# The second norm, moved from a stage of its own into the first output projection

## The chip, the cores and the metric

The kernel runs on 1 core of one Trainium2 chip. The metric is the device time of one execution in microseconds; several executions are run and their median is taken.

## The reference

Two blocks of a model, one after the other, on a sequence of 2048 rows of width 1024. The place that matters is the seam between them:

```
mix = concatenate([dn, sw], axis=-1)             # 2048 x 1024, delta rule and windowed attention
x1  = x + mix @ w_out                            # end of the first block
h   = rmsnorm(x1, norm_g)                        # start of the second block
proj = h @ w_in2                                 # 1024 -> 6144 columns
...                                              # chunked attention, convolution, gates
return rmsnorm(x1 + m @ w_out2, final_norm_g)
```

All is float32. Each product is done as three passes over a rounded part (`hi`) and the rest (`lo`): hi·hi, hi·lo, lo·hi.

## The kernel before, in words

The program is a chain of stages (blocks) that run one after the other on all engines; at the end of a block all engines meet, its semaphores are cleared, and the next begins. Each engine follows its own list of instructions and waits on semaphores. The order of the work is written out by hand.

`mix_output` (tiles `mo_*`) is the first output projection. It works on 16 tiles of 128 rows, two buffers of each tile. For a tile, GpSimd adds the two directions of the delta rule, squares them, and gates the window attention; VectorE and ScalarE norm, weight and gate the rows into `mix`; TensorE turns `mix` by 4 transposes (`turn`) into `pt`; ScalarE rounds it into `mhi` (`split_hi`); VectorE takes the rest into `mlo` (`split_lo`); TensorE does 48 products of 512 columns into `pp`; VectorE adds `x`; SyncE stores the row tile to `x1` in memory and loads the next `x`. ScalarE issues the five loads of rows three tiles ahead (`load_rows`, two of `delta_o`, one each of `gate_rows`, `sw_fm`, `gate_fm`) between its `split_hi` and its `root`. VectorE's order in a step is `split_lo(i+1)`, `rows(i+2)`, the sum of `pp` and `x` for tile i.

`norm_combine` (tiles `n_*`) is the second norm. It reads `x1` back, norms each row tile (a square with its sum on ScalarE, a root, a reciprocal, one scaling on VectorE into `xs`), turns it by 8 transposes of TensorE, and joins two tiles that stand 512 rows apart (a pair) into the 7 forms `A11, A12, A22, S1, S3, S2, S4` of a seven-product matrix scheme. Four pairs (`STORED`, the second half of the sequence) go to memory in `h_later`, 1792 KB each. The other four (`KEPT`) are for the first half. All pass through a buffer `cb`, two of them, and are rounded into `chi` and `clo` (the trace's `h_hi`, `h_lo`). It also loads the first weights and splits the first of them.

`project_second` (tiles `pj_*`) is the projection that follows: 24 units of 2 x 512 rows-by-columns blocks, each unit 7 steps of 12 products. Its first product of a unit, `B11`, uses form `A11`. For unit 0, ScalarE and VectorE split the weights of the 7 steps ahead of their accumulating work.

Of the kernel before, what the change touches and what calls it, by code (L numbers as in the profile page):

```python
# [27 lines left out]
F32 = mybir.dt.float32  # L28
# [1849 lines left out]
def attention(nc, name, warm, n_warm, consts, load_tile, n_kt, bias_of, bias_shape, load_bias, sink_rows, lanes, shapes, span, deep, out,  # L1878
# [14 lines left out]
    with Ctx(nc, name, USED) as c:  # L1893
# [4 lines left out]
        kr = c.sb("kr", [P, nk_tiles, SEQ])  # L1898
        vr = c.sb("vr", [P, TILES, vw])
        neg = [c.sb(f"neg{k}", [P, kp]) for k in SLOTS]  # L1900
        pr = [[c.sb(f"pr{r}{k}", [P, kp]) for k in SLOTS] for r in S]
# [89 lines left out]
        def _(sp):  # L1991
# [7 lines left out]
            if later:  # L1999
                w_out, delta_o, gate_rows, norm_row, ident_src = later.sources  # L2000
                for s in S:
                    for d in range(2):
                        sp.dma_start(later.of[s][:, d, :], delta_o[d, s]).then_inc(delta_in[s], 16)
# [9 lines left out]
            if later:  # L2013
# [3 lines left out]
                for s in S:  # L2017
                    sp.dma_start(later.gate[s][:], gate_rows[s]).then_inc(row_const_in, 16)
# [281 lines left out]

class MixAhead:


    def __init__(self, nc, stack, w_out, delta_o, gate_rows, norm_row, consts):
# [4 lines left out]
        self.raw = sb("raw", [P, KT, DM])  # L2309
        self.whi = sb("whi", [P, KT, DM], F32R)  # L2310
        self.wlo = sb("wlo", [P, KT, DM], F32R)
# [13 lines left out]
def mix_output(nc, delta_o, sw_fm, gate_rows, gate_fm, ahead, x, out, warm):  # L2325

    W = DN_W  # L2330
    with Ctx(nc, "mo", USED) as c:
        S = range(2)
        ident, wrow, whi, wlo = ahead.ident, ahead.wrow, ahead.whi, ahead.wlo
        of, gate, st = ahead.of, ahead.gate, ahead.st
        mix = [c.sb(f"mix{s}", [P, W]) for s in S]
# [4 lines left out]
        mlo = [c.sb(f"mlo{s}", [P, KT, P], F32R) for s in S]  # L2340
        pt = [c.ps(f"pt{s}", [P, W]) for s in S]
# [3 lines left out]
        names = ("rows_in x_in summed2 squared summed eps_added rooted inverted normed weighted gated sw_gated turned hi_ready lo_ready product added stored").split()  # L2345
        m = {n: c.sems(n, 2) for n in names}
        block = c.open_block()
        H = TILES // 2

        def load_rows(eng, j, t):  # L2350

            i, s, u = of_pair(j, t)
            for d in range(2):
                eng.dma_start(of[s][:, d, :], delta_o[d, i]).then_inc(m["rows_in"][s], 16)
            eng.dma_start(gate[s][:], gate_rows[i]).then_inc(m["rows_in"][s], 16)
            load_window(eng, j, t)

        def load_window(eng, j, t):
            i, s, u = of_pair(j, t)
            at = bass.ds(i * P, P)  # L2360
# [3 lines left out]
        def load_x(sp, j, t):  # L2364
            i, s, u = of_pair(j, t)
            sp.dma_start(xin[s][:], x[i]).then_inc(m["x_in"][s], 16)

        @block.sync
        def _(sp):
            def step(j, t, follow):  # L2370
                i, s, u = of_pair(j, t)
                sp.wait_ge(m["added"][s], u + 1 + START)
                sp.dma_start(out[i], xin[s][:]).then_inc(m["stored"][s], 16)
                if follow > 1:
                    sp.wait_ge(m["stored"][s], 16 * u + 16 + START)
                    load_x(sp, j, t + 2)

            for t in range(2):
                load_window(sp, 0, t)
            for t in range(2):  # L2380
                load_x(sp, 0, t)
            tile_pairs(sp, step)
            for s in S:
                sp.wait_ge(m["stored"][s], 16 * H + START)

        @block.gpsimd
        def _(pool):
            for s in S:
                pool.wait_ge(m["rows_in"][s], 32 + START)
                nc.gpsimd.tensor_tensor(sw[s][:], sw[s][:], gsw[s][:], ALU.mult).then_inc(m["sw_gated"][s], 1)  # L2390
            with pool.Fori(1, H) as j:
                for s in S:
                    pool.wait_ge(m["rows_in"][s], 80 * j + 32 + START)
                    nc.gpsimd.tensor_tensor(of[s][:, 0, :], of[s][:, 0, :], of[s][:, 1, :], ALU.add).then_inc(
                        m["summed2"][s], 1)
                    pool.wait_ge(m["summed2"][s], j + START)
                    nc.gpsimd.tensor_tensor(of[s][:, 1, :], of[s][:, 0, :], of[s][:, 0, :], ALU.mult).then_inc(
                        m["squared"][s], 1)
                    nc.gpsimd.tensor_tensor(sw[s][:], sw[s][:], gsw[s][:], ALU.mult).then_inc(m["sw_gated"][s], 1)

        @block.vector
        def _(dve):
            def rows(j, t):

                i, s, u = of_pair(j, t)
# [7 lines left out]
                scale_rows(j, t)  # L2413

            def scale_rows(j, t):
                i, s, u = of_pair(j, t)
# [14 lines left out]
            def split_lo(j, t):  # L2431
                i, s, u = of_pair(j, t)
# [6 lines left out]
            def step(j, t, follow):  # L2439
                i, s, u = of_pair(j, t)  # L2440
                if follow > 0:
                    split_lo(j, t + 1)
                if follow > 1:
                    rows(j, t + 2)
                dve.wait_ge(m["product"][s], u + 1 + START)
                dve.wait_ge(m["x_in"][s], 16 * u + 16 + START)
# [1285 lines left out]
```

## Time and profile before

| | us |
|---|---|
| median of 3 runs | 3168.65 |
| the 3 runs | 3168.65, 3153.8, 3176.06 |
| the profiled execution, its own time | 3165.56 |
| its span | 3163.8 |
| TensorE busy in the span | 2940.3 (93%) |
| VectorE / ScalarE / GpSimd busy | 1795.2 / 1283.3 / 551.5 |

The mean granted TensorE clock of that execution is 0.971 of full speed. The profiled execution's time is the span plus 1.8 us around it. Busy times are of each engine by itself; the stage is what counts, since the stages follow one another.

### The profile page before, as it was taken

The numbers are of one execution on the slowest core, as the hardware profiler recorded it, in microseconds if no ns is written. First come the engines' busy times: TensorE is split into PE (matmuls) and PEld (weight loads), VectorE is DVE, ScalarE is ACT, GpSimd is POOL, SyncE is SP. The second block draws the span as 40 slices with busy tenths as digits, with TensorE's granted clock in tenths as the row PEclk, the third lists the DMA queues.
The fourth block names the chain that finished last, engine by engine and source line by source line (L and its number), as shares of the span: only waits on it lengthen the run. The fifth ranks groups of instructions, "written<-read, shape, count | busy, mean of one in ns | idle before, by whom it ended". The sixth has DMA issues, their size and how long they took to land. (4 is left out here: it accounts for less than half of the span.)

```text
span 3163.8 us, 56622 instructions
## 1 busy us (share of the span) xinstructions
PE 2940.3 (93%) x21119; PEld 2408.9 (76%) x21139; DVE 1795.2 (57%) x3274; ACT 1283.3 (41%) x2752; POOL 551.5 (17%) x475
## 2 busy tenths in 40 slices
PE   7998999997999989899599999999999899989998
PEld 6886998775888866688388888878888666668787
DVE  5755443074877857554755775665775455543433
ACT  5221433154665569410523223433223377730232
POOL 0000000062343400132032232342332100000000
PEclk9999999999998999999799999999999999999999
DMA  4221775154666532354633223443223362145443
GB/s 141 80 80 73 247 256 200 52 153 161 198 199 192 157 113 98 113 203 153 228 107 107 70 70 117 160 140 106 65 71 116 114 199 88 30 158 207 173 146 119
DMA packets 302666, 431.96 MB, mean 137 GB/s; under 512 B 43600, under 2 KB 181072, under 8 KB 296784
## 3 DMA queue, kind: packets, MB, share of 16 engines
q1 hardware_dynamic: 253936, 392.40, 37.5%
q10 hardware_dynamic: 48480, 36.18, 3.6%
q8 instruction: 162, 2.65, 0.3%
q14 instruction: 88, 0.72, 0.1%
HBM read 279.01 MB, written 149.49 MB: 135 GB/s over the span
## 5 line engine op out<-in xcount | busy, mean ns | idle before, releaser
L114 PE MATMUL pj_pp<-h_hi,pj_whi 128*128 128x512 f32 x1152 | 449.9, 391 | 6.9 <-POOL h_lo L3121 6.9
L115 PE MATMUL pj_pp<-h_lo,pj_whi 128*128 128x512 f32 x1152 | 448.7, 390 | 0.0
L116 PE MATMUL pj_pp<-h_hi,pj_wlo 128*128 128x512 f32 x1152 | 448.7, 389 | 0.0
L114 PEld LDWEIGHTS pj_pp<-h_hi,pj_whi 128*128 128x128 f32 x1152 | 216.6, 188 | 52.8 <-issue 8.1
L2948 ACT CAST pj_whi<-w_raw 128x512 fp32r<-128x512 f32 x192 | 119.1, 622 | 327.1 <-PE pj_pp L116 318.5
L116 PEld LDWEIGHTS pj_pp<-h_hi,pj_wlo 128*128 128x128 f32 x1152 | 216.6, 188 | 45.0
L115 PEld LDWEIGHTS pj_pp<-h_lo,pj_whi 128*128 128x128 f32 x1152 | 216.7, 188 | 44.8
L3012 DVE TENSOR_TENSOR pj_wlo<-w_raw,pj_whi 128x512 fp32r<-128x512 f32 x192 | 159.7, 832 | 11.6 <-ACT pj_whi L2948 8.6
L114 PE MATMUL np_pp<-h_hi,np_whi 128*128 128x512 f32 x384 | 150.4, 392 | 0.0
L116 PE MATMUL np_pp<-h_hi,np_wlo 128*128 128x512 f32 x384 | 149.7, 390 | 0.0
L115 PE MATMUL np_pp<-h_lo,np_whi 128*128 128x512 f32 x384 | 149.7, 390 | 0.0
L3141 POOL TENSOR_TENSOR w_raw<-w_raw,pj_t 128x512 f32<-128x512 f32 x48 | 62.7, 1306 | 441.6 <-DVE pj_wlo L3012 441.6
L2948 ACT CAST pj_whi<-pj_t 128x512 fp32r<-128x512 f32 x96 | 59.6, 621 | 173.7 <-PE pj_pp L116 155.0
L1689 POOL TENSOR_TENSOR gr_sw<-gr_tab,gr_wrow 128x64 f32<-128x64 f32 x32 | 15.7, 521 | 641.8 <-DMA gr_ident<-in_consts 641.8
L2227 ACT ACTIVATE ca_pr<-ca_neg,ca_nmx 128x640 f32<-128x640 f32 (+4 forms) x128 | 97.7, 763 | 67.3 <-DVE ca_nmx L2167 67.3
L2167 DVE CUSTOM_DVE_ANT_0 ca_neg<-ca_s,ca_bias 128x640 f32<-128x640 f32 (+4 forms) x128 | 89.8, 739 | 51.1 <-PE ca_s L2051 49.5
L345 DVE SCALAR_TENSOR_TENSOR np_acc<-np_pre,np_taps,np_acc 128x2048 f32<-128x2048 f32 (+3 forms) x60 | 115.5, 1926 | 2.1
L114 PE MATMUL mo_pp<-ahead_whi,mo_mhi 128*128 128x512 f32 x256 | 103.3, 404 | 0.5 <-DVE mo_mlo L2451 0.5
L115 PE MATMUL mo_pp<-ahead_wlo,mo_mhi 128*128 128x512 f32 x256 | 101.9, 398 | 0.0
L116 PE MATMUL mo_pp<-ahead_whi,mo_mlo 128*128 128x512 f32 x256 | 101.9, 398 | 0.0
L114 PE MATMUL fo_pp<-fo_whi,fo_mhi 128*128 128x512 f32 x256 | 99.8, 390 | 0.0
L116 PE MATMUL fo_pp<-fo_whi,fo_mlo 128*128 128x512 f32 x256 | 99.6, 389 | 0.0
(415 smaller groups left out, 7174.4 us busy)
## 6 DMA issues: line engine op xcount, KB each, us to landing
w_raw<-in_w_second SPq DMA_DIRECT2D x192, 256.0 KB, 2.8
ds_pk<-scratch_pack SPq DMA_DIRECT2D x64, 384.0 KB, 4.6
scratch_pack<-rp_out SPq DMA_DIRECT2D x32, 512.0 KB, 2.7
ds_pk<-scratch_pack SPq DMA_DIRECT2D x64, 256.0 KB, 3.7
scratch_sig_fm<-pj_ob SPq DMA_DIRECT2D x64, 256.0 KB, 2.2
mb_sg<-scratch_sig_fm SPq DMA_DIRECT2D x16, 1024.0 KB, 7.7
rp_fm<-scratch_qkv_fm SPq DMA_DIRECT2D x96, 128.0 KB, 2.8
scratch_qkv_fm<-np_acc SPq DMA_DIRECT2D x11, 1024.0 KB, 4.8
```

The source lines that it names most:

```text
L114: nc.tensor.matmul(out, ah, bh, start=(first and i == 0), stop=False)
L115: nc.tensor.matmul(out, ah, bl, start=False, stop=False)
L116: mm = nc.tensor.matmul(out, al, bh, start=False, stop=(last and i == n - 1))
L345: nc.vector.scalar_tensor_tensor(out=acc[s][:, at], in0=pre[s][:, at.start + t:at.stop + t], scalar=taps[:, n, t:t + 1], in1=acc[s][:, at] ...
L1689: ins = nc.gpsimd.tensor_tensor(sw[s][:, :, k, a:a + HH], tab[s][:, 1, :, a:a + HH], wrow[:, k, b:b + HH].unsqueeze(1).to_broadcast([P, 2, ...
L2167: nc.vector.tensor_tensor_reduce(neg[k][:, 0:n * P], s_ps[k][:, 0:n * P], bias_of(bias, h)[:, b0:b0 + n * P], -scale, sink[:, 1, h:h + 1] ...
L2227: nc.scalar.activation(pr[q % 2][k][:, 0:n * P], neg[k][:, 0:n * P], ACT.Exp, bias=nmx[s][:, h:h + 1], scale=-1.0, accum_out=den[s][:, 0, ...
L2948: nc.scalar.copy(whi[i], raw_of[i]).then_inc(hi_ready[i], 1)
L3012: nc.vector.tensor_tensor(wlo[i], raw_of[i], whi[i].bitcast(F32), ALU.subtract).then_inc(lo_ready[i], 1)
L3141: nc.gpsimd.tensor_tensor(raw[1][0], raw[1][0], t2[:], ALU.subtract).then_inc(t4_ready, 1)
```

## The change

`mix_output` and `norm_combine` become one block, `mix_and_norm`. The row tiles are taken in a new order, `ROW_ORDER`, so that two tiles 512 rows apart follow each other, the second half of the sequence first. Each tile of x1 is squared, rooted and scaled from the sum that stands in `xin`, and TensorE turns it in the step after its own, between the 36th and the 37th product. The sum of `pp` and `x` is made in two halves. There is one `xs`, one `nt` in PSUM and one `cb`. `S2` and `S4` go from VectorE to GpSimd. The kept pairs are written in full precision into `combos`, and no longer rounded there, but for `A11`; the other six forms are rounded in `project_second`, ahead of the first unit, with half of the rest on GpSimd. All loops over tiles are written out. Large tiles of the stages share a hand-placed region (`Arena`), in which the window attention before has its tiles too.

```diff
-def mix_output(nc, delta_o, sw_fm, gate_rows, gate_fm, ahead, x, out, warm):
-def norm_combine(nc, name, x, norm_row, consts, chi, clo, later, w_first, w_raw, w_split, warm):
+ROW_ORDER = [8 * half + p + 4 * e for half in (1, 0) for p in range(4) for e in range(2)]
+def mix_and_norm(nc, delta_o, sw_fm, gate_rows, gate_fm, ahead, arena, x, norm_row, w_first, later, out, warm):
+    STORED_PAIRS = H // 2
...
+        xs = c.sb("xs", [P, DM])
+        cb = c.sb("cb", [P, N_COMB, K4W, P])
+        nt = c.ps("nt", [P, KT, P])
...
+        def forms(u, k):
+            return cb[:, k] if u < STORED_PAIRS else combos[:, k, place(u)]
         @block.sync
+            def store_forms(u):
+                sp.wait_ge(low_ready, u + 1 + START)
+                sp.wait_ge(s4_ready, u + 1 + START)
+                sp.dma_start(later[:, :, place(u)], cb[:]).then_inc(later_stored, 16)
+            def step(i):
+                s, u = i % 2, i // 2
+                if i >= 3 and i % 2 and (i - 3) // 2 < STORED_PAIRS:
+                    store_forms((i - 3) // 2)
                 sp.wait_ge(m["added"][s], u + 1 + START)
+                sp.dma_start(out[ROW_ORDER[i]], xin[s][:]).then_inc(m["stored"][s], 16)
+                if i + 2 < TILES:
+                    sp.wait_ge(xs_ready, i + 1 + START)
                     sp.wait_ge(m["stored"][s], 16 * u + 16 + START)
+                    load_x(i + 2)
         @block.gpsimd
+            def last_forms(u):
+                pool.wait_ge(s1_ready, u + 1 + START)
+                pool.wait_ge(top_ready, u + 1 + START)
+                nc.gpsimd.tensor_tensor(forms(u, S2), forms(u, S1), forms(u, A11), ALU.subtract).then_inc(s2_ready, 1)
+                pool.wait_ge(s2_ready, u + 1 + START)
+                nc.gpsimd.tensor_tensor(forms(u, S4), forms(u, A12), forms(u, S2), ALU.subtract).then_inc(s4_ready, 1)
+            for i in range(2, TILES):
...                                  # sum, square and gate of tile i, as before
+                if i % 2 and i >= 5:
+                    last_forms((i - 5) // 2)
+            last_forms(H - 2)
+            last_forms(H - 1)
         @block.vector
+            def low_forms(u):
+                dve.wait_ge(row_turned, 2 * u + 2 + START)
+                dve.wait_ge(a22_ready, u + 1 + START)
+                nc.vector.tensor_tensor(forms(u, S1), nt[:, 0:K4W, :], forms(u, A22), ALU.add).then_inc(s1_ready, 1)
+                dve.wait_ge(top_ready, u + 1 + START)
+                nc.vector.tensor_tensor(forms(u, S3), forms(u, A11), nt[:, 0:K4W, :], ALU.subtract).then_inc(low_ready, 1)
+            def norm(i):
...                                  # scale and epsilon, wait for the root, reciprocal, then
+                nc.vector.scalar_tensor_tensor(out=xs[:], in0=xin[s][:], scalar=nst[:, 3:4], in1=nrow[:], op0=ALU.mult,
+                                               op1=ALU.mult).then_inc(xs_ready, 1)
+            def step(i):
+                if i >= 3 and i % 2:
+                    low_forms((i - 3) // 2)
+                if i + 1 < TILES:
+                    split_lo(i + 1)
+                if 1 <= i <= TILES:
+                    norm(i - 1)
+                if i + 2 < TILES:
+                    rows(i + 2)
+                if i < TILES:
+                    add_x(i)
...
+            for h in S:              # after step(TILES + 1)
...
+                nc.vector.tensor_tensor(clo[:, A11, 2 * h:2 * h + 2], combos[:, A11, 2 * h:2 * h + 2],
+                                        chi[:, A11, 2 * h:2 * h + 2].bitcast(F32), ALU.subtract)
         @block.scalar
+            def copy_row(i):
+                u = i // 2
+                act.wait_ge(row_turned, i + 1 + START)
+                if i % 2 == 0:
+                    if 0 < u <= STORED_PAIRS:
+                        act.wait_ge(later_stored, 16 * u + START)
...                                  # A11 and A12 of pair u out of nt
+                else:
+                    nc.scalar.copy(forms(u, A22), nt[:, K4W:KT, :]).then_inc(a22_ready, 1)
+            def step(i):
+                if i >= 2:
+                    copy_row(i - 2)
+                if i + 1 < TILES:
+                    split_hi(i + 1)
+                if 1 <= i <= TILES:
+                    square(i - 1)
+                if i + 3 < TILES:
+                    act.wait_ge(m["lo_ready"][(i + 1) % 2], (i + 1) // 2 + 1 + START)
+                    load_rows(act, i + 3)
+                if 1 <= i <= TILES:
+                    norm_root(i - 1)
+                if i + 2 < TILES:
+                    root(i + 2)
         @block.tensor
+            def turn_row(i):
+                u = i // 2
+                pe.wait_ge(xs_ready, i + 1 + START)
...                                  # and top_ready or low_ready, then 8 transposes of xs into nt
+            def step(i):
+                s, u = i % 2, i // 2
+                if i + 1 < TILES:
+                    turn(i + 1)
                 pe.wait_ge(m["lo_ready"][s], u + 1 + START)
                 pe.wait_ge(m["added"][s], u + START)
+                products(i, 0, range(0, KT)).then_inc(half_product, 1)
+                products(i, NCOL, range(0, 4))
+                turn_row(i - 1)
+                products(i, NCOL, range(4, KT)).then_inc(m["product"][s], 1)
...
+            pe.wait_ge(m["half_added"][0], H + START)
+            keep_warm(nc, pp[0][:, 0:NCOL], warm, 20)
+            turn_row(TILES - 1)
 def project_second(...):
         # ScalarE, ahead of the first unit
             for i in range(1, STEPS):
+                for h in S:
+                    nc.scalar.copy(chi[:, A_OF[i], 2 * h:2 * h + 2], combos[:, A_OF[i], 2 * h:2 * h + 2]).then_inc(first_hi, 1)
                 split_hi(i, 0)
         # VectorE
             for i in range(1, STEPS):
+                for h in S if i == 1 else S[0:1]:
+                    dve.wait_ge(first_hi, 2 * (i - 1) + h + 1 + START)
...                                  # clo of that half
                 split_lo(i, 0)
         # GpSimd, first unit: the other half of clo
+            def first_low_of(i):
+                pool.wait_ge(first_hi, 2 * i + START)
...
+                if u == 0:
+                    for i in range(2, 4):        # after t1, t2, t3
+                        first_low_of(i)
+                if u == 0:
+                    for i in range(4, STEPS):    # after t4
+                        first_low_of(i)
         # TensorE, step(u, i)
+                if u == 0 and i > 0:
+                    pe.wait_ge(first_lo, i + 1 + START)
+                if u == 0 and i > 1:
+                    pe.wait_ge(first_low, i - 1 + START)
```

## Rows read from the trace of the kernel before

**Rows 1.** Stretches: length; busy PE, PEld, DVE, ACT, POOL; TensorE clock, DMA share, GB/s.

```profile
1327.00:1503.00 176.00, 176.00 (x776) 142.88 (x774) 83.63 (x121) 18.16 (x41) 49.17 (x39) 0.98 0.51 176
...
1512.00:1585.40 73.40, 40.74 (x213) 25.52 (x214) 59.12 (x79) 44.06 (x71) 3.75 (x3) 0.78 0.65 226
```

**Rows 2.** Timeline of VectorE and TensorE at both ends of the norm stage (start, length).

```profile
1503.13 1.22 DVE L2447 TENSOR_TENSOR mo_xin<-mo_pp,mo_xin 128x1024 f32<-128x1024 f32 x1 [9.91 <-PE mo_pp L116]
...
1577.29 1.22 DVE L2685 TENSOR_TENSOR h_lo<-n_cb,h_hi 128x1024 fp32r<-128x1024 f32 x1
...
1585.40 0.58 PE L114 MATMUL pj_pp<-h_hi,w_hi 128*128 128x512 f32 x1
```

**Rows 3.** Groups of instructions, 1500 to 1590 (busy us, mean ns; idle before, releaser).

```profile
L2673 DVE SCALAR_TENSOR_TENSOR n_xs<-n_x,n_stat,n_wrow 128x1024 f32<-128x1024 f32 x16 | 19.8, 1282 | 0.3
L2727 PE MATMUL n_pt<-n_ident,n_xs 128*128 128x128 f32 x128 | 19.3, 301 | 17.9 <-DVE n_xs L2673 17.8
L2625 ACT ACTIVATE n_xs<-n_x 128x1024 f32<-128x1024 f32 x16 | 16.9, 1059 | 31.3 <-DMA n_x<-scratch_x 31.1
...
L2649 ACT COPY n_cb<-n_pt 128x1024 f32<-128x1024 f32 x8 | 8.0, 1000 | 5.1 <-DMA scratch_h_later<-n_cb 3.3 <-DVE h_lo L2679 1.8
...
L2701 DVE TENSOR_TENSOR n_cb<-n_pt,n_cb 128x512 f32<-128x512 f32 x8 | 5.5, 687 | 2.3 <-ACT n_cb L2654 2.1
...
L2679 DVE TENSOR_TENSOR h_lo<-n_cb,h_hi 128x1024 fp32r<-128x1024 f32 x4 | 4.9, 1219 | 0.0
```

**Rows 4.** Timeline of a steady step of the projection, engine by engine (ACTq: issues).

```profile
1399.04 0.60 PE L2499 MATMUL mo_pt<-ahead_ident,mo_mix 128*128 128x128 f32 x4
1399.40 0.48 PE L114 MATMUL mo_pp<-ahead_whi,mo_mhi 128*128 128x512 f32 x1
...
1410.64 0.60 PE L2499 MATMUL mo_pt<-ahead_ident,mo_mix 128*128 128x128 f32 x4
...
1399.34 1.23 DVE L2447 TENSOR_TENSOR mo_xin<-mo_pp,mo_xin 128x1024 f32<-128x1024 f32 x1 [2.80 <-PE mo_pp L116]
...
1400.16 0.62 ACT L2472 CAST mo_mhi<-mo_sw 128x512 fp32r<-128x512 f32 x1
...
1402.29 0.87 ACTq L2354 DMA_DIRECT2D ahead_of<-scratch_delta_o  x2
...
1404.80 0.20 ACT L2464 ACTIVATE ahead_st<-ahead_st 128x4 f32<-128x4 f32 x1 [4.01 <-issue]
...
1406.70 0.69 DVE L2429 TENSOR_TENSOR mo_mix<-mo_mix,ahead_gate 128x512 f32<-128x512 f32 x1
...
1413.10 1.20 DVE L2436 TENSOR_TENSOR mo_mlo<-mo_sw,mo_mhi 128x512 fp32r<-128x512 f32 x1
```

**Rows 5.** DMA issues: 1300 to 1600, then two stores by themselves (KB, us to landing).

```profile
scratch_h_later<-n_cb SPq DMA_DIRECT2D x4, 1792.0 KB, 7.3
...
scratch_h_later<-n_cb SPq DMA_DIRECT2D x1, 1792.0 KB, 9.0
...
scratch_h_later<-n_cb SPq DMA_DIRECT2D x1, 1792.0 KB, 6.4
```

**Rows 6.** Timeline: TensorE behind three of its waits, and VectorE after the first.

```profile
1326.70 1.11 PE L2499 MATMUL mo_pt<-ahead_ident,mo_mix 128*128 128x128 f32 x4 [4.36 <-DVE mo_mix L2429]
...
1341.28 1.23 DVE L2447 TENSOR_TENSOR mo_xin<-mo_pp,mo_xin 128x1024 f32<-128x1024 f32 x1 [4.87 <-PE mo_pp L116]
...
2064.18 0.47 PE L114 MATMUL pj_pp<-h_hi,pj_whi 128*128 128x512 f32 x1 [2.85 <-POOL h_lo L3121]
...
2070.11 0.76 PE L114 MATMUL pj_pp<-h_hi,pj_whi 128*128 128x512 f32 x1 [2.96 <-POOL h_lo L3121]
```

**Rows 7.** Stretches of 1 and 4 us behind those waits (columns as in Rows 1).

```profile
1331.00:1332.00 1.00, 1.00 (x4) 0.78 (x3) 0.76 (x2) 0.00 (x0) 0.00 (x0) 0.50 0.44 61
...
2070.00:2074.00 4.00, 3.89 (x10) 3.11 (x11) 1.42 (x3) 0.62 (x1) 3.92 (x3) 0.58 0.36 126
```

**Rows 8.** Instructions of one line, GpSimd on 1024 columns (min/median/max ns).

```profile
L3121 POOL TENSOR_TENSOR h_lo<-pj_araw,h_hi x7: 2344/2399/3260, 2033.1 to 2067.6; 128x1024 fp32r<-128x1024 f32 x7
```

More of the change, by code:

```diff
@@ L2017, in _ @@
                 for s in S:
-                    sp.dma_start(later.gate[s][:], gate_rows[s]).then_inc(row_const_in, 16)
+                    sp.dma_start(later.gate[s][:], gate_rows[ROW_ORDER[s]]).then_inc(row_const_in, 16)
                 sp.wait_ge(raw_in, 16 + START)
@@ L2380, in _ @@
-            for t in range(2):
-                load_x(sp, 0, t)
-            tile_pairs(sp, step)
+                    load_x(i + 2)
+                if i == TILES - 4:
+                    for r in S:
+                        for q in S:
+                            sp.dma_start(w_raw[r][q], w_first[q][:, r * K4W:(r + 1) * K4W, :]).then_inc(
+                                w_ahead if r or q else w0_in, 16)
+            for i in range(2):
+                load_window(sp, i)
+            for i in range(2):
+                load_x(i)
@@ L2488, in _, with turn @@
             act.wait_ge(m["lo_ready"][0], 1 + START)
-            load_rows(act, 0, 2)
-            tile_pairs(act, step, peel=2)
+            load_rows(act, 2)
+            for i in range(TILES + 2):
+                if i == TILES - 1:
+                    act.wait_ge(w0_in, 16 + START)
+                    nc.scalar.copy(w_split[0], w_raw[0][0]).then_inc(w0_hi, 1)
+                if i == TILES + 1:
+                    for s in S:
+                        act.wait_ge(m["product"][s], H + START)
+                    for h in S:
+                        nc.scalar.copy(chi[:, A11, 2 * h:2 * h + 2], combos[:, A11, 2 * h:2 * h + 2]).then_inc(a11_hi, 1)
+                step(i)
         @block.tensor
         def _(pe):
-            def turn(j, t):
-                i, s, u = of_pair(j, t)
+            def turn(i):
+                s, u = i % 2, i // 2
                 pe.wait_ge(m["gated"][s], u + 1 + START)
@@ L2519, in _ @@
                 if ks.start:
-                    turn(0, 1)
+                    turn(1)
                     pe.wait_ge(m["lo_ready"][0], 1 + START)
                 for a in (0, NCOL):
-                    mm = split_products(nc, pp[0][:, a:a + NCOL],
-                                        [(mhi[0][:, k, :], mlo[0][:, k, :], whi[:, k, a:a + NCOL],
-                                          wlo[:, k, a:a + NCOL]) for k in ks], first=ks.start == 0, last=ks.stop == KT)
+                    mm = products(0, a, ks)
@@ L2731 @@
+            for i in range(1, TILES):
+                step(i)
+            pe.wait_ge(m["half_added"][0], H + START)
+            keep_warm(nc, pp[0][:, 0:NCOL], warm, 20)
+            turn_row(TILES - 1)
 STEPS = 7
@@ L2741, in second_units, with project_second @@
     return ["qk"] * 4 + ["v"] * 2 + ["z"] * 2 + conv + ["sig"] * 8
-def project_second(nc, w_tiles, conv_w, consts, chi, clo, later, raw, w_split, qk, v_rows, z, yconv, sig, warm):
+def project_second(nc, w_tiles, conv_w, consts, combos, chi, clo, later, raw, w_split, qk, v_rows, z, yconv, sig, warm):
     KINDS = second_units()
@@ L3573, in build @@
     x1 = scratch("x1", [TILES, P, DM])
-    with ExitStack() as held:
-        ahead = MixAhead(nc, held, d["w_out1"], delta_o, gate_rows, d["dn_norm"], d["consts"])
-        if stage("wa"):
-            window_attention(nc, d, rope_fm, proj_rows, sw_fm, ahead, warm)
-        if stage("mix"):
-            mix_output(nc, delta_o, sw_fm, gate_rows, gate_fm, ahead, d["x"], x1, warm)
     h_later = scratch("h_later", [P, N_COMB, 4, K4W, P])
```

449 lines of the change are left out of this document (175 added, 274 removed).

## The prediction

> **What bounds the kernel now.** I read the busy shares first, then stretches cut at the borders of the stages, then the timeline of one steady step, then the waits. In the output projection TensorE is busy for the whole of 1327 to 1503, 176.00 of 176.00 us; VectorE has 83.63, ScalarE 18.16 and GpSimd 49.17 [rows 1]. So there anything that costs TensorE no time is free, and what it must do or wait for is paid in full. In the norm stage TensorE is not the bound: VectorE is busy for 59.12 of 73.40 us and ScalarE for 44.06, and part of TensorE's 40.74 is only there to keep it warm [rows 1]. Between VectorE's last sum of the projection (1503.13) and the first product of the next one (1585.40) lie 82.3 us [rows 2]. This is all that the change can win. Its price is paid in the projection before and at the border behind.
>
> **The border, after.** Time 0 is the start of the last half sum, at the place of 1503.13. Half sum 0.7 (as a form of 512 columns, 0.69); square 1.06 and the read-out of its sum [rows 3], to 2.0; scale and epsilon, root (0.20 [rows 4]), reciprocal, with the hand-overs to 2.65; scaling into `xs` 1.28 [rows 3], to 3.95. Twenty warming products cover TensorE until about 4.4. Eight transposes 0.9, to 5.3. ScalarE has rounded the two halves of `A11` meanwhile (two of 1.0, off the path) and copies `A22`, 0.6, to 5.95. VectorE makes `S1` and `S3`, 0.69 each less their overlap [rows 3], to 7.25, then two rests of `A11`, 1.22 each [rows 3], to 9.7; GpSimd's `S2` and `S4` end with it (1.3 each, a little over half of its 2.40 for 1024 columns [rows 8]). From the end of the last rest (1577.29 + 1.22) to the first product there are 1585.40 - 1578.51 = 6.9 us [rows 2], a change of stage that I keep. So 16.6 us in place of 82.3: **-65.7**.
>
> **Eight transposes in each step.** Four transposes take 0.36 us to the next product (1399.04 to 1399.40); that product stands 0.08 longer, and the step is 1410.64 - 1399.04 = 11.60 us, so 48 products stand 0.234 apart [rows 4]. Eight cost 2 x 0.36 + 0.08 = 0.8; the upper bound is the norm stage's 19.3 / 16 = 1.2 us a tile, part of them at a low clock [rows 3]. I take 0.9. Fifteen lie inside the projection (the last is in the border): **+13.5** (12 to 18). The step becomes 12.5 us, and the transposes are wanted 0.44 + 36 x 0.234 = 8.8 us after its start.
>
> **Is `xs` there by then?** In a step, counted from its first transpose: the half sum is done at 1.0 (the sum starts at 0.30 now), ScalarE's two casts end at 1.75 [rows 4], its square at 2.9. VectorE's two rests end at 3.1; beside a gate of GpSimd's, the second is 1.20 instead of 0.69 [rows 4], and they end at 3.7. In every second step `S1` and `S3` come first, 1.3 us, of which 0.7 was idle: 4.1. Only then does ScalarE issue its five loads, 1402.29 to the root at 1404.80, 2.5 us [rows 4], and behind those stands the root of the second norm. Issues end at 5.7 to 6.8, root and reciprocal at 6.2 to 7.3, `xs` at 7.5 to 8.7. So it is in time, by 0.1 to 1.3 us. Behind it on VectorE stand the rows of tile i+2, reduce to gate: some 4.1 us: now the root starts at 1404.80 and the gate ends at 1407.39, 2.6 us on [rows 4]; reduce, scale and the root itself before it are 1.5. They end at 11.6 to 12.8 where the step ends at 12.5. The steps with `S1` and `S3` are the tight ones, seven of them, 0.3 us each: **+2** (0 to 6).
>
> On the extra subtractions of GpSimd the Trainium skill speaks against the change: its page "GPSIMD Engine Reference", section "8. Key points", has GpSimd contend with VectorE instructions that have two SBUF inputs. The 1.20 us beside 0.69 agrees. By that rule the scaling into `xs` (two SBUF inputs) would also grow if `S2` and `S4` last into it, to about twice, and seven steps would lose up to 1 us more each; the forecast holds without it.
>
> **Where I see the largest cost: one `cb`.** Pair u is complete in step 2u+3, and `copy_row` of pair u+1 is the first thing that ScalarE does in step 2u+4; it waits for the store of pair u. The store is SyncE's, and behind `load_x` of tile 2u+4, which waits for `xs` of tile 2u+2, made in step 2u+3 at 7.5 to 8.7. GpSimd's `S4` is done at 6.5 to 8. So the store is issued at about 8.8, with 512 KB of x just ahead and row loads in flight. Landing took 6.4 us by itself and 9.0 with loads of x beside it, median 7.3 [rows 5]. I take 8.5: 17.3, which is 4.8 into step 2u+4. Before, there were two buffers, and such a wait came to 3.3 us in all [rows 3]. Queued behind it on ScalarE stand the copy (1.0), the casts of tile 2u+5, the square, the five issues and the root; `xs` is ready 8.05 behind the landing, at 12.85, and TensorE wants it at 8.8. It waits 4.05 us.
>
> **And its clock.** After a wait of 4.36 us, four transposes took 1.11 instead of 0.60 us, and the stretch at 1331 still shows half the clock (1.2 GHz); the step took 1341.28 - 0.30 - 1326.70 = 14.3 us, 2.7 more than 11.60 [rows 4, 6, 7]. After one of 2.85 us the next product still took 0.47; after one of 2.96, 0.76 and a clock of 0.58 in that stretch [rows 6, 7]. So a wait of 4 us most likely brings the low clock, and I add 2.5. This happens for pairs 1, 2, 3 and 4, in steps 4, 6, 8 and 10: 4 x (4.05 + 2.5) = **+26.2**. Ends: landing in 6.4 leaves waits of 2 us and no loss of clock, 8; landing 2.5 later than I take gives 4 x 9.3 = 37.
>
> **The first unit behind.** In `project_second`, ScalarE rounds two halves of a form (1.0 each [rows 3]) and a weight (0.62 [rows 4], less the overlap) for each of six steps, 2.5 us a step where TensorE needs 12 x 0.234 = 2.8; VectorE has a rest of 1.22 and one of 0.69 [rows 3]. GpSimd's half rest is 2.40 us (up to 3.26) [rows 8], five of them and four weight sums of 1.3: with the wait of its fourth sum for `lo_ready` of B21 its last ends some 22.5 after the last rest before the border. TensorE starts at 6.9 and wants the last at 23.7. So there is 1.2 to spare; with the longer durations it is late by up to 4: **+1.5** (0 to 5).
>
> Nothing is won by the reads of x1 that fall away, since they lay in the stage that is gone. Loops written out, more semaphores, the new order and the shared memory I take at nothing: TensorE covers the first; without that cover they'd be tenths of a us.
>
> **The sum.** -65.7 + 13.5 + 2 + 26.2 + 1.5 = -22.5; 3165.56 - 22.5 = 3143 for a profiled execution. The median stands 3.1 above that execution, so I say 3146. The three runs spread by 0.35% to each side, so 1% (31.7 us) is about what can be told from no change.
>
> **Rivals.** A: the store lands early enough, or the clock stays up. Waits of 2 us instead of 4.05 and no low clock: +8 instead of +26, 3128; with the transposes at 0.8, 3126. For it: 6.4 us alone, and two of four stores of before were waited for little. Against: 0.5 MB ahead in the same queue. B: the steps without a store are late too, since `xs` has 0.1 us to spare in the worst of them. 1.5 us in each of eleven steps: +16.5, 3163. C, slower: ScalarE's five issues take 5 us instead of 2.5, as the queue is fuller by 1792 KB for two tiles. Then `xs` comes at 11 in every step, 2.3 us late and at the edge of the low clock: 11 x (2.3 + 2.5) + 4 x 2.3 = +62, 3208. It decides from issues of about 4.5 us; against it, they are 2.5 at a DMA share of 0.51 [rows 1, 4]. D: the change doesn't do what it says, and the border is only halved, to 41 us, because another thing than the last tile's chain (SyncE's wait for its stores or the first weights) opens the next stage: +24, 3170. Against: the last pair that is stored is done four tiles before the end, and a store of `x1` is 512 KB.
>
> Page "DMA: Bandwidth & Descriptors", section "Queues, rings and completion order", of the Trainium skill says that descriptors of a ring are consumed in order. By it the x load goes before the store, which alone would make 9.0 rather than 7.3; no row here shows the order itself.
>
> **Chances.** Forecast 0.50, A 0.25, B 0.13, C 0.08, D 0.04. Faster by over 1% (under 3137): most of A and a fifth of the forecast, 0.32. Slower by over 1%: C and little else, 0.09. Same: 0.59. The range goes from A with the low ends of the other terms (3123, and 5 less for the spread of the runs) to B with a high end of the store's term (3174).
>
> **What would show it.** Right: ScalarE's copy of `A11` waits for the DMA of `h_later` four times, some 5 us; TensorE's transposes out of `xs` wait for VectorE behind it, some 4 us, with a clock near 0.5 after; steps of 12.5 us otherwise; 16 to 17 us from the last sum to the first product. Wrong: waits in all steps (B, C), or none (A). I'd be wrong most easily by the landing of the store, on which 29 us hang.

## The result, and the profile after

| | before | after |
|---|---|---|
| median, 6 runs each | 3159.66 us | 3133.11 us |
| ratio, 95% interval | 1 | 0.9918 (0.989 to 0.9946) |
| profiled execution (span) | 3165.56 (3163.8) | 3128.35 (3126.6) |

The change made the kernel 26.5 us faster, 0.8% (17 to 35 us by the interval). Run twice more below, it came out 18.4 and 25.7 us below the kernel before. The forecast was 22.5 less than before; its absolute figure, 3146, started from a median of three runs of 3168.65, where six runs give 3159.66. The two profiled executions are 37 us apart, but 9.7 us of that had arisen before the stage that the change rewrites: the first product of the projection starts at 1310.45 in the one and at 1300.79 in the other. Ahead of it the change touches only where the tiles of the window attention stand, and in the second run of the changed kernel the same product starts at 1310.80. So what follows compares stretches with known ends, not spans.

The steps of the projection come first, as the timeline of TensorE shows them (`turn` is L2677, `turn_row` L2688). They answer to [rows 4].

```profile
1343.08 0.60 PE L2677 MATMUL mo_pt<-ahead_ident,mo_mix 128*128 128x128 f32 x4
1351.88 1.03 PE L2688 MATMUL mo_nt<-ahead_ident,mo_xs 128*128 128x128 f32 x8
1355.55 0.60 PE L2677 MATMUL mo_pt<-ahead_ident,mo_mix 128*128 128x128 f32 x4
1368.57 1.97 PE L2688 MATMUL mo_nt<-ahead_ident,mo_xs 128*128 128x128 f32 x8 [4.06 <-DVE mo_xs L2555]
1374.97 0.60 PE L2677 MATMUL mo_pt<-ahead_ident,mo_mix 128*128 128x128 f32 x4
...
1387.47 0.60 PE L2677 MATMUL mo_pt<-ahead_ident,mo_mix 128*128 128x128 f32 x4
1399.76 1.09 PE L2688 MATMUL mo_nt<-ahead_ident,mo_xs 128*128 128x128 f32 x8 [3.31 <-DVE mo_xs L2555]
1405.02 0.66 PE L2677 MATMUL mo_pt<-ahead_ident,mo_mix 128*128 128x128 f32 x4 [1.39 <-DVE mo_mix L2530]
```

Step 3 (1343.08 to 1355.55) is 12.47 us, 0.87 more than 11.60. Its transposes out of `xs` start 8.80 after its own start and wait for nothing. Step 4 is 19.42: 4.06 of waiting for `xs`, then transposes at 1.97 instead of 1.03, which is half the clock (0.50 granted), and half-speed products behind. Step 6 is 17.55: 3.31 of waiting, no fall of the clock, and 1.39 of waiting at its end for the mix of tile 8. Steps 8 and 10 are 18.96 and 18.07, with waits of 3.66 and 3.82. In step 10 the transposes still take 1.09, and the clock falls only behind them:

```profile
1461.76 1.09 PE L2688 MATMUL mo_nt<-ahead_ident,mo_xs 128*128 128x128 f32 x8 [3.82 <-DVE mo_xs L2555]
...
1463.57 0.63 PE L114 MATMUL mo_pp<-arena_whi,mo_mhi 128*128 128x512 f32 x1
...
1466.80 0.39 PE L116 MATMUL mo_pp<-arena_whi,mo_mlo 128*128 128x512 f32 x1
```

The granted clock is 0.50 from 1464 to 1466, and the step loses 1.8 us beyond its wait (18.07 - 12.47 - 3.82). So a look at the first instructions behind a wait isn't enough to say that the clock stayed up. The four steps stand 24.1 us above four ordinary ones: 14.8 of waiting for `xs`, 7.9 behind the waits (2.89, 0.38, 2.83 and 1.78), 1.4 of waiting for the mix. The eight ordinary steps from 2 to 13 are 12.46 to 12.52.

The waits of the whole stretch, 1290 to 1560 (us in total, times, longest), tell who is late for whom.

```profile
ACT mo_cb L2623 <- DMA scratch_h_later<-mo_cb: 26.3, 3, 8.9
...
PE mo_nt L2688 <- DVE mo_xs L2555: 14.9, 4, 4.1
...
ACT arena_combos L2623 <- DMA scratch_h_later<-mo_cb: 9.0, 1, 9.0
```

ScalarE stands four times for the store of the pair before, 35 us in all, where it stood for 3.3 before [rows 3]; TensorE waits 14.9 us behind that. In step 6 the chain is this, from the timelines of SyncE (steps 3 and 4), ScalarE and VectorE.

```profile
1351.12 0.33 SPq L2442 DMA_DIRECT2D mo_xin<-in_x  x1
1351.55 0.61 SPq L2447 DMA_DIRECT2D scratch_h_later<-mo_cb  x1
...
1392.21 1.01 ACT L2623 COPY mo_cb<-mo_nt 128x1024 f32<-128x1024 f32 x1 [8.63 <-DMA scratch_h_later<-mo_cb]
1393.12 0.59 ACT L2612 CAST mo_mhi<-mo_pt 128x512 fp32r<-128x512 f32 x1
...
1395.59 0.82 ACTq L2429 DMA_DIRECT2D ahead_of<-scratch_delta_o  x2
...
1397.98 0.20 ACT L2636 ACTIVATE mo_nst<-mo_nst 128x1 f32<-128x1 f32 x1 [2.70 <-issue]
...
1398.41 1.28 DVE L2555 SCALAR_TENSOR_TENSOR mo_xs<-mo_xin,mo_nst,mo_nrow 128x1024 f32<-128x1024 f32 x1
```

The store of pair 0 is issued 8.5 us into step 3, right behind the load of x; the one that step 6 waits for, of pair 1, is issued 8.0 into step 5 (1382.99). Four such stores landed 9.1 to 9.5 us after their issue (median 9.3), which answers to [rows 5]. In step 6 the copy starts at 1392.21, 4.7 into the step; the casts, the square, the five issues and the root follow in a row, and `xs` is there 7.5 us on.

The border to the next stage, VectorE and TensorE, answers to [rows 2].

```profile
1529.13 0.69 DVE L2565 TENSOR_TENSOR mo_xin<-mo_pp,mo_xin 128x512 f32<-128x512 f32 x1 [5.74 <-PE mo_pp L116]
...
1536.22 4.12 DVE L2598 TENSOR_TENSOR arena_clo<-arena_combos,arena_chi 128x1024 fp32r<-128x1024 f32 x2
...
1547.32 0.99 PE L114 MATMUL pj_pp<-arena_chi,arena_w_hi 128*128 128x512 f32 x1
```

It is 18.2 us from the last half sum to the first product, where 82.3 were. The two rests at its end took 4.12 us, not 2.4.

The first unit of `project_second` grew: its second unit starts at 1574.03, 26.7 us after its first, where it was 1604.67 - 1585.40 = 19.3. Groups of instructions from 1547 to 1574:

```profile
L3132 POOL TENSOR_TENSOR arena_clo<-arena_combos,arena_chi 128x1024 fp32r<-128x1024 f32 x5 | 14.3, 2881 | 1.4 <-ACT arena_chi L2976 1.4
L3076 DVE TENSOR_TENSOR arena_clo<-arena_combos,arena_chi 128x1024 fp32r<-128x1024 f32 x5 | 10.4, 2087 | 0.0
L114 PE MATMUL pj_pp<-arena_chi,pj_whi 128*128 128x512 f32 x24 | 10.3, 428 | 4.7 <-POOL arena_clo L3132 3.8 <-DVE pj_wlo L3014 0.9
...
L3014 DVE TENSOR_TENSOR pj_wlo<-arena_w_raw,pj_whi 128x512 fp32r<-128x512 f32 x4 | 7.9, 1980 | 0.2 <-ACT pj_whi L2948 0.2
```

Rests of 1024 columns took 2.09 us on VectorE on average (1.22 in [rows 3]) and 2.88 on GpSimd (2.40 in [rows 8]); the four rests of 512 columns that read `arena_w_raw` took 1.98 on average where 0.69 is their time alone. By the view of the whole stretch (1547.3 to 1574), VectorE was busy for 23.0 of 26.7 us and GpSimd for 21.7; TensorE waited 4.7 us and lost some more to the clock, which was 0.91 on average:

```profile
1547.30:1574.00 26.70, 22.00 (x86) 17.34 (x85) 23.00 (x14) 14.45 (x19) 21.73 (x11) 0.91 0.16 49
```

### The profile page after: what moved, and what is told of

It is laid out like the page before. It is cut to its first block and busy times, and to the rows that moved or that the text cites. A ratio compares the mean times of both kernels' runs of the same rounds, so it can differ in the third digit from the quotient of the medians.

```text
span 3126.6 us, 56243 instructions
## 1 busy us (share of the span) xinstructions
PE 2918.1 (93%) x21061; PEld 2395.2 (77%) x21077; DVE 1808.6 (58%) x3287; ACT 1284.8 (41%) x2762; POOL 589.8 (19%) x496
## 3 DMA queue, kind: packets, MB, share of 16 engines
q8 instruction: 166, 2.72, 0.4%
## 5 line engine op out<-in xcount | busy, mean ns | idle before, releaser
L114 PE MATMUL pj_pp<-arena_chi,pj_whi 128*128 128x512 f32 x1152 | 450.8, 391 | 8.5 <-POOL arena_clo L3132 3.8
L115 PE MATMUL pj_pp<-arena_clo,pj_whi 128*128 128x512 f32 x1152 | 449.5, 390 | 0.0
L116 PE MATMUL pj_pp<-arena_chi,pj_wlo 128*128 128x512 f32 x1152 | 449.3, 390 | 0.0
L114 PEld LDWEIGHTS pj_pp<-arena_chi,pj_whi 128*128 128x128 f32 x1152 | 216.9, 188 | 55.1 <-issue 10.4
L116 PEld LDWEIGHTS pj_pp<-arena_chi,pj_wlo 128*128 128x128 f32 x1152 | 217.1, 188 | 45.2
L115 PEld LDWEIGHTS pj_pp<-arena_clo,pj_whi 128*128 128x128 f32 x1152 | 217.2, 189 | 44.9
L2948 ACT CAST pj_whi<-arena_w_raw 128x512 fp32r<-128x512 f32 x192 | 119.2, 622 | 319.1 <-PE pj_pp L116 303.4
L3014 DVE TENSOR_TENSOR pj_wlo<-arena_w_raw,pj_whi 128x512 fp32r<-128x512 f32 x192 | 166.9, 869 | 9.8 <-ACT pj_whi L2948 7.1
L1689 POOL TENSOR_TENSOR gr_sw<-gr_tab,gr_wrow 128x64 f32<-128x64 f32 x32 | 15.8, 522 | 642.5 <-DMA gr_ident<-in_consts 642.5
L114 PE MATMUL mo_pp<-arena_whi,mo_mhi 128*128 128x512 f32 x256 | 106.5, 416 | 0.5 <-DVE mo_mlo L2582 0.5
L3014 DVE TENSOR_TENSOR arena_w_lo<-arena_w_raw,arena_w_hi 128x512 fp32r<-128x512 f32 x47 | 66.4, 1414 | 65.7 <-ACT arena_w_hi L2948 65.7
L116 PE MATMUL mo_pp<-arena_whi,mo_mlo 128*128 128x512 f32 x256 | 103.4, 404 | 0.0
```

The lines of the kernel that those rows point to most:

```text
L114: nc.tensor.matmul(out, ah, bh, start=(first and i == 0), stop=False)
L115: nc.tensor.matmul(out, ah, bl, start=False, stop=False)
L116: mm = nc.tensor.matmul(out, al, bh, start=False, stop=(last and i == n - 1))
L1689: ins = nc.gpsimd.tensor_tensor(sw[s][:, :, k, a:a + HH], tab[s][:, 1, :, a:a + HH], wrow[:, k, b:b + HH].unsqueeze(1).to_broadcast([P, 2, ...
L2948: nc.scalar.copy(whi[i], raw_of[i]).then_inc(hi_ready[i], 1)
L3014: nc.vector.tensor_tensor(wlo[i], raw_of[i], whi[i].bitcast(F32), ALU.subtract).then_inc(lo_ready[i], 1)
```

## The experiments

All kernels were run in five rounds against the kernel before. Each line below has its median, and its ratio to the kernel before with the interval.

| kernel | median us | ratio (95%) | long steps 4, 6, 8, 10 | first unit |
|---|---|---|---|---|
| the change again | 3141.36 | 0.9937 (0.9919 to 0.9954) | 19.3, 18.3, 15.8, 18.5 | 26.8 |
| four places | 3118.24 | 0.9861 (0.9833 to 0.9888) | 12.5 each | 28.4 |
| store first | 3121.85 | 0.9872 (0.985 to 0.9894) | 15.9, 15.0, 14.4, 15.1 | 26.7 |
| warmed waits | 3138.16 | 0.9925 (0.9908 to 0.9942) | 16.2, 17.6, 19.5, 16.9 | 26.5 |
| no fourth wait | 3132.67 | 0.9905 (0.988 to 0.993) | 17.3, 15.1, 18.3, 12.5 | 26.8 |
| root first | 3121.25 | 0.988 (0.9852 to 0.9907) | 14.7, 13.7, 13.7, 13.2 | 26.7 |
| turned twice | 3153.37 | 0.9978 (0.996 to 0.9996) | 18.6, 18.0, 17.8, 19.4 | 28.4 |
| rests on VectorE | 3133.04 | 0.9913 (0.9889 to 0.9936) | 18.4, 17.8, 17.4, 18.1 | 21.6 |
| the change, third time | 3137.56 | 0.9926 (0.9905 to 0.9946) | 16.2, 18.2, 17.8, 18.0 | 26.7 |
| S2, S4 on VectorE | 3143.70 | 0.9944 (0.9923 to 0.9965) | 20.1, 18.6, 20.2, 18.5 | 26.4 |
| combined | 3109.42 | 0.9853 (0.9828 to 0.9877) | 12.5 each | 23.9 |

The steps and the unit are read from the timeline of TensorE of one profiled execution each. Single steps differ by 1 to 3 us from one execution to the next of the same kernel, so the long steps are compared as a sum. The first unit is 26.4 to 28.4 in the ten executions whose code for it is that of the change.

**The change again.**

> The changed kernel again, as the reference for the three beside it. Four waits of TensorE for xs of 3 to 4 us in steps 4, 6, 8 and 10, some 24 us over four ordinary steps of 12.5 us; some 26 us faster than the kernel before.

The waits hold: four of 2.98 to 4.11 us for `xs`, 14.1 in all, and four steps 22.1 us above ordinary ones. The time does not: 18.4 us below the kernel before, not 26.

**Four places.**

```diff
-            return cb[:, k] if u < STORED_PAIRS else combos[:, k, place(u)]
+            return combos[:, k, place(u)]
...
-                    if 0 < u <= STORED_PAIRS:
-                        act.wait_ge(later_stored, 16 * u + START)
+                    if u >= STORED_PAIRS:
+                        act.wait_ge(later_stored, 16 * (u - STORED_PAIRS + 1) + START)
```

> The stored pairs are written into the four places of combos, which lie idle then, so that no pair waits for the store of the one before. Theory (the wait of ScalarE for the one cb makes the four long steps): no wait of TensorE for xs is left, steps 4, 6, 8 and 10 fall to 12.5 us, and the kernel is 24 us faster than the changed one. Rival (the long steps come from the load on VectorE and GpSimd, and the store only happens to stand there): waits of 2 us or more stay and it gains under 8.

It came out 23.1 us below the changed kernel of the same comparison (0.9861 against 0.9937, and the intervals are apart). Of TensorE's waits from 1340 to 1500 this is the whole list:

```profile
PE mo_pt L2677 <- DVE mo_mix L2530: 0.8, 1, 0.8
```

No wait for `xs` is left, and steps 3 to 13 are 12.46 to 12.68. The four long steps alone are 22.0 us shorter. The load on VectorE and GpSimd is the same, so the rival falls.

**Store first.** SyncE's order in a step:

```diff
-                if i >= 3 and i % 2 and (i - 3) // 2 < STORED_PAIRS:
-                    store_forms((i - 3) // 2)
                 sp.wait_ge(m["added"][s], u + 1 + START)
                 sp.dma_start(out[ROW_ORDER[i]], xin[s][:]).then_inc(m["stored"][s], 16)
+                if i >= 2 and i % 2 == 0 and (i - 2) // 2 < STORED_PAIRS:
+                    store_forms((i - 2) // 2)
```

> SyncE issues the store of pair u before it waits for xs and loads x of tile 2u+4; one cb as before. Theory (the landing counts from an issue that SyncE's own order holds back until xs is there): the issue moves from 8.3 to some 3 to 5 us after the start of step 2u+3, the landing by the same 4 us, and of the four long steps most of 24 us goes: 15 to 22 faster than the changed kernel. Rival (the landing is bound by the traffic of row loads, not by the issue): the landing takes as much longer as it starts earlier, and it gains under 5. x of tile 2u+4 now lands behind 1792 KB and might come late for the sum; then it is less.

19.5 us below the changed kernel by the medians. The four long steps account for 11.6 of it (60.4 us against 72.0), less than the forecast's 15 to 22; of the 15.1 us between the two profiled executions, 5.0 had arisen before the projection. SyncE's timeline in step 3, which starts at 1350.35 here, and ScalarE's copy in step 4, which starts at 1362.84:

```profile
1355.33 0.61 SPq L2447 DMA_DIRECT2D scratch_h_later<-mo_cb  x1
1358.54 0.33 SPq L2442 DMA_DIRECT2D mo_xin<-in_x  x1
...
1365.21 1.02 ACT L2623 COPY mo_cb<-mo_nt 128x1024 f32<-128x1024 f32 x1 [5.66 <-DMA scratch_h_later<-mo_cb]
```

The issue is at 5.0 in the step instead of 8.5, the landing takes 9.8 instead of 9.3 (medians), and the copy starts at 2.4 in step 4. The waits for `xs` fall to 0.98 to 1.82, and none brings the low clock; the mix is late at five steps' ends, 3.6 us in all. So SyncE's order alone held the store back by 3 to 3.5 us, and the landing took only 0.5 longer for it. The load of x behind the store landed after 8.0 us instead of 5.3, and VectorE didn't wait for it.

**Warmed waits.**

```diff
+                if i in (4, 6, 8, 10):
+                    pe.wait_ge(m["added"][1 - s], (i - 1) // 2 + 1 + START)
+                    keep_warm(nc, pp[1 - s][:, 0:NCOL], warm, 12)
                 turn_row(i - 1)
```

> Twelve warming products (2.7 us) in steps 4, 6, 8 and 10, in the place where TensorE waits for xs. The waits for xs stay (less 2.7 us each as idle time), and only the clock is different. Theory (two or three of the four waits bring the low clock, at 2 to 2.5 us each): 5 to 7 us faster than the changed kernel, no transposes of 1.97 us. Rival (the clock is not what lengthens those steps): no change, or up to 2 us slower where a wait is shorter than the warming.

3.2 us below the changed kernel, with intervals that overlap: by the times alone it is not settled. In the trace three of the four transposes behind the waits take 1.09 or 1.10 and one 1.97:

```profile
1398.36 1.09 PE L2688 MATMUL mo_nt<-ahead_ident,mo_xs 128*128 128x128 f32 x8 [1.53 <-DVE mo_xs L2555]
...
1429.84 1.97 PE L2688 MATMUL mo_nt<-ahead_ident,mo_xs 128*128 128x128 f32 x8 [2.80 <-DVE mo_xs L2555]
```

The forecast of 5 to 7 us is missed. What the steps lose beyond their waits falls from 8.0 us in the changed kernel beside it to 2.5, so the clock gave back some 5.5; but the idle times of this run and the warming in front of them (2.7 us) come to 16.2 us, 2.1 more than the waits beside it, and three waits for the mix at the steps' ends take 1.6. That the clock adds to the long steps is shown by the steps themselves. In the three runs of the changed kernel, nine of the twelve have a stretch at a granted clock of 0.50 and stand 1.6 to 3.0 us above an ordinary one beyond their waits; the three others stand 0.2 to 0.4 above it, as 15.84 - 12.47 - 3.15.

**No fourth wait.**

```diff
-                    if 0 < u <= STORED_PAIRS:
+                    if 0 < u < STORED_PAIRS:
```

> ScalarE's wait for the fourth store, in step 10, is left out: pair 4 goes to combos, not to cb, so nothing needs it. Theory: step 10 falls from 18 to 12.5 us and the other three stay, 5 to 6 us faster than the changed kernel. Rival (something else makes that step long): step 10 stays.

Step 10 is 12.46 in this run; the other three stay at 15 to 18. By the times it is 7 to 10 us faster than the changed kernel (0.9905 against 0.9926 and 0.9937), with intervals that overlap, so this is read from the step. A fourth of the cost stood for a wait that protects nothing.

**Root first.**

```diff
+                if 1 <= i <= TILES:
+                    norm_root(i - 1)
                 if i + 3 < TILES:
                     act.wait_ge(m["lo_ready"][(i + 1) % 2], (i + 1) // 2 + 1 + START)
                     load_rows(act, i + 3)
-                if 1 <= i <= TILES:
-                    norm_root(i - 1)
```

> ScalarE does the root of the second norm before it issues the five loads of rows, no longer behind them. Theory (ordinary steps have xs in time, and only the four long ones wait): xs comes 2.4 us earlier, which shortens the four waits by so much each and takes the low clock off some: 10 to 15 us faster than the changed kernel, ordinary steps still 12.5. Rival (the loads are what the rows of the next tiles wait for, and come later now): new waits for the rows in ordinary steps, no gain.

0.988, some 16 us below the changed kernel. The waits for `xs` are 1.99, 1.01, 1.04 and 0.46, and none brings the low clock; the four steps sum to 55.3 us instead of 72.0. One wait of 0.65 us for the mix appears, too small to count. Of the 16.7, 9.6 are the waits (4 x 2.4), and the rest is the clock, which stays up behind all four.

This run also shows what the landing hangs on. Three of its four stores are issued 10.5 to 11.0 us into their step, once GpSimd's `S4` is done, which is some 2.5 later than in the changed kernel and 4 to 5 behind the load of x. They land after 6.5 to 6.7 us, and ScalarE's copy starts 4.3 to 4.8 into the next step, no later than before. The first, issued 0.4 behind that load, takes 11.1. So an issue moved by itself does not move the landing by as much: what is in flight then counts too.

**Turned twice.**

```diff
-                for k in range(KT):
+                for k in list(range(KT)) * 2:
```

> Each row tile of x1 is turned twice, into the same place: 8 transposes more in each step. Theory (transposes are paid in full on TensorE at 0.09 to 0.1 us each): ordinary steps of 13.2 to 13.3 instead of 12.47, some 12 us slower than the changed kernel. Rival (TensorE has room in the steps): ordinary steps stay at 12.5.

```profile
1485.78 0.60 PE L2677 MATMUL mo_pt<-ahead_ident,mo_mix 128*128 128x128 f32 x4
1494.58 1.91 PE L2688 MATMUL mo_nt<-ahead_ident,mo_xs 128*128 128x128 f32 x16
1499.12 0.60 PE L2677 MATMUL mo_pt<-ahead_ident,mo_mix 128*128 128x128 f32 x4
```

Ordinary steps are 13.34, 0.87 above 12.47, and the kernel is at 0.9978, 13 to 16 us above the changed one. The eight transposes are paid in full, at the price of the forecast.

**Rests on VectorE.**

```diff
-                for h in S if i == 1 else S[0:1]:
+                for h in S:
...
-                if u == 0:
-                    for i in range(4, STEPS):
-                        first_low_of(i)
```

> In the first unit of project_second, VectorE makes both halves of the rests of the six forms, and GpSimd none of them. Theory (the two engines hold each other up on operations with two SBUF inputs, 3.4 instead of 1.2 us on VectorE and 3.0 instead of 2.4 on GpSimd, and that makes the unit 26.7 us instead of 19.3): the rests fall to 1.2 us, and the unit to 20 to 22 us, though VectorE has more work: 4 to 7 us faster than the changed kernel. Rival (the work is simply too much, wherever it is done): the unit stays at 26 or grows, as VectorE has five rests of 1.2 us more.

Groups from 1546.8 to 1568.5:

```profile
L3076 DVE TENSOR_TENSOR arena_clo<-arena_combos,arena_chi 128x1024 fp32r<-128x1024 f32 x10 | 11.7, 1212 | 0.0
```

And the view of one line, one of GpSimd's sums of the weights (minimum, median and longest in ns, first and last start in us):

```profile
L3152 POOL TENSOR_TENSOR arena_w_raw<-arena_w_raw,pj_t x48: 1284/1288/6215, 1557.5 to 2455.1; 128x512 f32<-128x512 f32 x48
```

VectorE does ten rests in 11.7 us where it did five in 10.4, and the unit falls from 26.7 to 21.6. The one sum of this line that falls into the stretch, the first of the 48, took 6.2 us where their median is 1.3, so the two engines still hold each other up; it is only no longer what TensorE waits for. The kernel is 4 to 8 us faster than the changed one by the ratios (0.9913), which the intervals alone don't separate; the unit's 5.1 is read from the trace. The 21.6 is clear of the 26.4 to 28.4 of the executions with the change's own code, and the rival (too much work wherever it is done) falls.

**The change a third time**, and beside it **S2, S4 on VectorE**.

> The changed kernel once more, as the reference for the two beside it: 0.8% faster than the kernel before.

```diff
                 nc.vector.tensor_tensor(forms(u, S3), forms(u, A11), nt[:, 0:K4W, :], ALU.subtract).then_inc(low_ready, 1)
+                nc.vector.tensor_tensor(forms(u, S2), forms(u, S1), forms(u, A11), ALU.subtract).then_inc(s2_ready, 1)
+                nc.vector.tensor_tensor(forms(u, S4), forms(u, A12), forms(u, S2), ALU.subtract).then_inc(s4_ready, 1)
```

> S2 and S4 are back on VectorE, right behind S1 and S3; GpSimd only gates the mix. Theory (VectorE's chain to xs has about 1 us to spare in a step with S1 and S3, 7.8 against 8.9): with 1.3 us more in front xs comes at 9.1, TensorE waits 0.3 us in seven ordinary steps, and the store, which is issued behind xs, lands later for the long steps: 2 to 6 us slower than the changed kernel. Rival (the rule that GpSimd and VectorE hold each other up on operations with two SBUF inputs decides): VectorE's operations beside S2 and S4 get shorter, the last two rests of the block fall from 2.1 to 1.2 us each, and it is 1 to 4 us faster.

Both theories are right in a part. The last two rests take what they take alone, as the rival said:

```profile
1547.53 2.35 DVE L2598 TENSOR_TENSOR arena_clo<-arena_combos,arena_chi 128x1024 fp32r<-128x1024 f32 x2
```

But the four waits for `xs` are 5.01, 4.33, 4.76 and 4.18, for the store is issued behind `xs` and that comes later (9.2 to 9.3 us into the step, not 8.0 to 8.5), and the kernel is at 0.9944, 6.1 us by the medians above the changed one beside it; the intervals overlap in part. No waits of 0.3 us in the steps with `S1` and `S3` appeared: those steps are 12.5 with an exception of 13.3 behind each of two long ones.

**Combined**: four places, root first, and rests on VectorE.

> Three edits together: the stored pairs in the four places of combos, the root ahead of the loads, and both halves of the first unit's rests on VectorE. Theory (the costs are separate, and with the first edit there is no wait that the second could shorten): -23 and -5 and 0, some 28 us faster than the changed kernel and 1.7% faster than the kernel before. Rival (they share one cover, or the root in front makes new waits): under 20.

28.1 us below the changed kernel beside it, as expected, and at 0.9853 the fastest of all. No step from 3 on is longer than 12.49. Its first unit is 23.9, not 21.6; TensorE waited 2.2 us in it instead of 1.6, and its granted clock there was 0.93 instead of 0.97. Four places alone were at 0.9861 in another comparison, so how much the other two edits add to it is not told apart.

## Why the prediction was right

The time fell by 26.5 us where 22.5 were forecast. The mechanism stands term by term, but for one term that was mis-sized:

| term | forecast | the profile after |
|---|---|---|
| border | -65.7 | 18.2 - 82.3 = -64.1 |
| fifteen times eight transposes | +13.5 | 15 x (12.47 - 11.60) = +13.1 |
| ordinary steps late | +2 | 0 |
| four long steps | +26.2 | +24.1 |
| first unit | +1.5 | +7.4 |
| sum | -22.5 | -19.5 |

**The border** was as worked out, but for 1.6 us: the two last rests stood beside GpSimd's `S4` and took 4.12 instead of 2.35, as the run with `S2` and `S4` on VectorE shows. The 6.9 us from the last rest to the first product were 7.0 (1547.32 - 1540.34).

**The transposes** cost what was taken, 0.87 a tile against 0.9; turning twice confirmed it.

**The slack in ordinary steps** was judged too small in two places. TensorE found `xs` ready in all of them, also with two more forms on VectorE in front: the trace has it at 7.8 us against 8.8 in step 7, where the forecast had up to 8.7. The +2 itself stood for the mix of the next tile, which was to end at up to 12.8 in a step of 12.5. In the steps with `S1` and `S3` it ended at 11.2 to 12.1, so nothing was paid in this execution; the third run of the change waited for it in two early steps, 0.74 and 0.32.

**The single `cb`** was the largest cost, and its chain held in each link: store issued at 8.0 to 8.5 (8.8 was forecast), landing after 9.3 (8.5), copy 4.7 to 5.5 into the step (4.8), `xs` 7.5 behind it (8.05), TensorE's wait 3.31 to 4.06 (4.05). Only the sign for ScalarE, waits of some 5 us, was off: it was free earlier and stood for 8.6 to 9.0. The edit that takes only this wait away gained 23.1 us; an earlier issue of the store gained 19.5, of which its long steps show 11.6, and a shorter queue behind the wait some 16. These are three ways to shorten one chain, and they don't add up. The forecast's 26.2 were 16.2 of waits and 10 of clock; measured were 14.8 of waits, 7.9 behind them and 1.4 for the mix. The low clock came behind three of the four waits, not all; its price was 1.6 to 3.0 where it came.

**The first unit** is the term that was mis-sized: +1.5 (0 to 5) was forecast, and it measured +7.4. The step that failed is "So there is 1.2 to spare": it took VectorE's durations as they stand alone, and GpSimd's too, with 3.26 us as their worst. Side by side, rests of 1024 columns took 2.09 and 2.88 on average, and GpSimd waited 3.5 us for a rest of VectorE's in between. Its last rest ended 29.8 us after the last one before the border (1570.10 - 1540.34), where the forecast had 22.5 and let TensorE want it at 23.7. In the Trainium skill, "GPSIMD Engine Reference", section "8. Key points", says that the two contend on VectorE instructions with two SBUF inputs; the forecast weighed this for the scaling into `xs`, where it didn't matter, and not for the first unit, where it did. The trace agrees there (2.09 instead of 1.22).

The sum of the terms is 7 us short of the medians' difference and within its interval; it is 1 more than the 18.4 of the second run of the change. In these two executions some 3 us are found: the hand-over of forms in the middle of `project_second`, where TensorE waited 6.9 us before and 3.7 after. But that wait was 3.6 to 6.0 in the other kernels with this change, and the delta scan differed by 8 us with unchanged code; why they do was not studied, and what makes up the 7 us stays open. So that the total came within 4 us is in part luck: the 6 us that the first unit was taken too low are offset by the long and the ordinary steps, 2 us each, and by this remainder.

Of the rivals, A has the nearer absolute figure: the measured 3133 lies 5 from its 3128 and 13 from the forecast's 3146, of which 9 are the median before. As a difference it lies 4 from the forecast's 22.5 and 14 from A's 40.5. A is wrong in its first reason, for the store did not land early, and right in its second for one wait of the four. B and D did not occur. C did not either: from step 3 on the five issues took 2.4 to 2.5 us. But there the store always landed before them; where it was issued among them (store first), they took 2.6.

## What to carry to other kernels

When a stage is folded into another one that is bound by an engine, the folded work is paid only where that engine does or waits for it: a norm of sixteen tiles cost 13 us of transposes, and a buffer that was halved on the way cost 24. Follow a wait on a store from the buffer back through the queue that issues it: what the issuing engine waits for first, and what stands behind the waiting copy, each make the wait longer, and each can be moved. Work that two engines share on the same memory is not to be added up from their times alone.

## What the runs showed of the hardware

- VectorE and GpSimd side by side on operations with two inputs from SBUF: a rest of 1024 columns took up to 3.43 us on VectorE instead of 1.21, one of 512 up to 2.87 instead of 0.68, and one sum of 512 columns on GpSimd 6.2 us instead of 1.3. The 6.2 us began with five operations of VectorE in a row, 1557.38 to 1562.60, and ended 1.1 us behind them. Moving work off GpSimd made the same total faster (26.7 to 21.6 us).
- TensorE's waits for `xs` of 2.64, 3.15 and 3.31 us were followed by the full clock for the whole step; waits of 2.72, 2.80, 2.98 and 3.17 us, in other steps and runs, by a stretch at half the clock. So the length of a wait by itself did not decide it between these. Behind none of the waits below 2 us did it fall, and it fell behind all of 3.40 and more. In some steps it fell before TensorE began again, in others 1.2 to 1.4 us later (behind waits of 3.10, 3.17, 3.82 and 3.85), when the transposes had run at 1.09 us.
- A store of 1792 KB landed in 9.1 to 9.5 us right behind a load of 512 KB, in 9.6 to 10.4 when it went first, and in 6.5 to 6.7 when it was issued 4 to 5 us behind the load (root first); 11.1 is the longest. The load behind the store took 8.0 instead of 5.3.
